# Retention of a hybrid decoder step, rewritten: states in four row groups, old states over four column groups, halves swapped by DMA, tables loaded earlier

## The reference, cut to what matters

```python
x1, x2 = xf[..., :half], xf[..., half:]                    # rotary, on q and k
return jnp.concatenate([x1 * c - x2 * s, x1 * s + x2 * c], axis=-1)
...
qk = jnp.einsum('bhid,bhjd->bhij', q, k) * dmask[None]
inner = jnp.einsum('bhij,bhje->bhie', qk, v)
cross = jnp.einsum('bhid,bhde->bhie', q, state) * jnp.exp(lg * (idx + 1.0))[None, :, :, None]
k_dec = k * jnp.exp(lg * (c_len - 1.0 - idx))[None, :, :, None]
new_state = jnp.exp(lg * c_len)[None, :, :, None] * state + jnp.einsum('bhjd,bhje->bhde', k_dec, v)
...
o_r = rmsnorm(o_r).reshape(b, s, RET_V_W) * jax.nn.silu(rg.astype(jnp.float32))
```

## Time and profile before

| | |
|---|---|
| three runs, median | 3351.26 us |
| profiled execution, its own time | 3356.02 us |
| its span (first to last instruction) | 3353.8 us |
| mean granted TensorE clock | 0.947 |
| PE busy | 3095.2 us (92%) |
| DVE busy | 1820.4 us (54%) |
| ACT busy | 1257.0 us (37%) |

### The profile page before, as it was taken

One profiled execution on the slowest core, in us unless ns is written; L12 is line 12 of the kernel. 1 busy time (PEld: TensorE's weight loads), 2 busy tenths in 40 slices (PEclk: granted clock), 3 DMA queues, 4 the chain that ended last, 5 costly groups with the idle time before them and its releaser, 6 DMA issues. The chain is left out here.

```text
span 3353.8 us, 52494 instructions
## 1 busy us (share of the span) xinstructions
PE 3095.2 (92%) x20972; PEld 2873.7 (86%) x20972; DVE 1820.4 (54%) x2531; ACT 1257.0 (37%) x1380; POOL 1016.0 (30%) x551
## 2 busy tenths in 40 slices
PE   7999999896887798599989999999999999999998
PEld 6999999674787686599989999999999888888886
DVE  5444443333222100565365889987777567777664
ACT  5322232111443334343334444445445333333332
POOL 0000000001454353000323888977777201111000
PEclk9999999666999899799989999999999999999999
DMA  6545453333447652466775789999999878888764
GB/s 218 173 157 175 151 174 100 114 101 125 133 149 242 221 161 90 136 212 200 193 158 138 187 225 241 233 254 294 281 294 278 315 283 318 289 314 318 277 226 163
DMA packets 446856, 696.74 MB, mean 208 GB/s; under 512 B 30493, under 2 KB 343101, under 8 KB 419166
## 3 DMA queue, kind: packets, MB, share of 16 engines
q1 hardware_dynamic: 397374, 554.41, 53.3%
q10 hardware_dynamic: 40128, 73.42, 7.9%
q0 software_dynamic: 9216, 67.11, 5.3%
HBM read 628.01 MB, written 63.70 MB: 206 GB/s over the span
## 5 line engine op out<-in xcount | busy, mean ns | idle before, releaser
L2506 POOL TENSOR_TENSOR peer_uT_low<-peer_uT,peer_uT_high 128x1024 fp32r<-128x1024 f32 x256 | 615.6, 2429 | 262.0 <-ACT peer_uT_high L2533 261.4
L968 POOL TENSOR_TENSOR gate_low<-gate_raw,gate_high 128x512 fp32r<-128x512 f32 x192 | 244.5, 1300 | 1073.8 <-ACT gate_high L924 1073.8
L2406 PE MATMUL banks<-x_high,peer_uT_high 128*128 128x256 f32 x2048 | 497.6, 285 | 7.0 <-ACT peer_picks_T L2565 5.1
L2407 PE MATMUL banks<-x_low,peer_uT_high 128*128 128x256 f32 x2048 | 493.4, 282 | 0.0
L2406 PEld LDWEIGHTS banks<-x_high,peer_uT_high 128*128 128x128 f32 x2048 | 389.9, 190 | 7.9 <-ACT peer_uT_high L2533 5.0
L2407 PEld LDWEIGHTS banks<-x_low,peer_uT_high 128*128 128x128 f32 x2048 | 389.2, 190 | 0.0
L228 PE MATMUL banks<-x_high,win_high 128*128 128x288 f32 (+1 forms) x1312 | 349.1, 296 | 0.0
L229 PE MATMUL banks<-x_low,win_high 128*128 128x288 f32 (+1 forms) x1312 | 348.7, 295 | 0.0
L198 ACT ACTIVATE win_high<-win_raw 128x2048 fp32r<-128x2048 f32 x84 | 160.8, 1915 | 334.0 <-DVEq L191 329.2
L2533 ACT ACTIVATE peer_uT_high<-peer_uT 128x1024 fp32r<-128x1024 f32 x256 | 260.5, 1055 | 63.3 <-DVE peer_uT L2656 62.6
L2656 DVE STREAM_TRANSPOSE peer_uT<-peer_u 128x1024 f32<-128x1024 f32 x192 | 234.1, 1230 | 84.1 <-DMA peer_u<-in_peer_u_dram 53.5
(11 more groups left out here) (398 smaller groups left out, 6688.5 us busy)
## 6 DMA issues: line engine op xcount, KB each, us to landing
win_raw<-in_w_in_dram SPq DMA_DIRECT2D x38, 2048.0 KB, 8.1
peer_u<-in_peer_v_dram SPq DMA_DIRECT2D x64, 1024.0 KB, 5.5
peer_area<-in_peer_v_dram SPq DMA_DIRECT2D x64, 1024.0 KB
gate_raw<-in_w_in_dram SPq DMA_DIRECT2D x96, 512.0 KB, 4.0
peer_u<-in_peer_u_dram SPq DMA_DIRECT2D x192, 256.0 KB
peer_u<-in_peer_u_dram ACTq DMA_DIRECT2D x192, 256.0 KB
w_raw<-in_w_up_ret_dram SPq DMA_DIRECT2D x8, 2048.0 KB, 8.9
w_raw<-in_w_out_dram SPq DMA_DIRECT2D x8, 2048.0 KB, 8.8
```

Of the source, the lines that this page charges most:

```text
L968: pool.tensor_tensor(self.low[:, p % 2, c, :, :], self.raw[:, p % 4, :, c * P:(c + 1) * P], self.high[:, p % 2, c, :, :], ALU.subtract).th ...
L2406: pe.matmul(out, UH[:, c, k, :], XH[:, k, 0:DENSE], start=(k == 0), stop=False)
L2407: pe.matmul(out, UH[:, c, k, :], XL[:, k, 0:DENSE], start=False, stop=False)
L2506: pool.tensor_tensor(UL[:, m % 2, part, :], UT[:, m % 2, part, :], UH[:, m % 2, part, :], ALU.subtract).then_inc(low, 1)
```

## The change

The output is the same. The changes are these:

1. The nine tables are loaded at the end of `input_projections` (SP, behind the last weight load) into `branch_outputs`, which is free until the next branch. The semaphores are no longer restarted in blocks of their own: POOL starts the rest of them during the input projection and renews the used ones during retention.
2. The silu of the gate runs at the end of ScalarE's part of the input projection.
3. Rotary: two DMAs a head copy q and k with their halves swapped into `SW`; VectorE multiplies by signed sines. There is no rotation matrix and no product for it. The factor on k goes into the decay tables.
4. v is turned straight from `Z`. The new tokens' k and v are turned four times into four groups of 32 output partitions, as ordinary products with the identity.
5. The old states become the moving operand (256 columns), q of the new tokens the stationary one (32 columns, zero but for the request's four). Four requests go to four column groups. The sum over requests needs a ScalarE copy (`CR`) and two small products with `pick`.
6. The new tokens' states run in four row groups of 32 partitions, each into its own bank, all eight before the first addition. The additions overwrite the old states in place; these are then stored, and the next load into that buffer waits for the store.
7. The root and the scaling are done head by head.
8. VectorE's order in head h is: the request's q (`QG`), the decayed keys (`KD`, `KDN`), the decayed scores (three pieces), the mean square of head h-1, the rotary sum of head h+1, the gate of head h, the four additions to the states, the scaling of head h-1. ScalarE copies the values (`V`, `V4`), `CR` and `PST`, squares the outputs, then takes the root of head h-1.
9. The heads are unrolled. PSUM banks 6 and 7 stay free, and the four first gate loads are issued at the start of retention. `TICKS_RETENTION` is (0, 0): no gate work runs in it.

```diff
+                def swap(h):
+                    if h >= 2:
+                        sp.wait_ge(qk_ready, after(h - 1))
+                    for half in range(2):
+                        sp.dma_start(SW[half * 64:half * 64 + 64, h % 2, :, :],
+                                     qk_z[64 - half * 64:128 - half * 64, h]).then_inc(swapped[h % 2], 16)
+                def load(h):
+                    if h >= 2:
+                        sp.wait_ge(new_stored[h % 2], after(16 * (h // 2)))
+                    sp.dma_start(ST[:, h % 2, :, :], state_in[h]).then_inc(state_loaded[h % 2], 16)
+                swap(0)
+                swap(1)
+                load(0)
+                gates.begin(sp)
+                load(1)
+                for h in range(RET_HEADS):
+                    gates.sp(sp, BEFORE)
+                    if h >= 1 and h + 1 < RET_HEADS:
+                        load(h + 1)
+                    if h + 2 < RET_HEADS:
+                        swap(h + 2)
...
+                def root(h):
+                    act.wait_ge(ms_ready, after(h + 1))
+                    act.activation(Z[:, RK + h, :], Z[:, RQ + h, :], ACT.Ln).then_inc(logs, 1)
+                    act.wait_ge(logs, after(h + 1))
+                    act.activation(Z[:, RV + 2 * h, :], Z[:, RK + h, :], ACT.Exp, scale=-0.5).then_inc(rstd_ready, 1)
+                for h in range(RET_HEADS):
+                    act.wait_ge(v_turned, after(h + 1))
+                    act.wait_ge(states_done, after(h))
+                    act.activation(V[:], PS[:, 1, :].rearrange("p (t e) -> p t e", t=2), ACT.Copy)
+                    act.activation(V4[:], PS[:, 2, 0:RET_DV], ACT.Copy).then_inc(v_ready, 1)
...
+                    act.wait_ge(cross_done, after(h + 1))
+                    act.activation(CR[:], PS[:, 0, 0:RET_DV], ACT.Copy).then_inc(cr_ready, 1)
+                    act.wait_ge(pstate_done, after(h + 1))
+                    act.wait_ge(pstate_stored, after(16 * h))
+                    act.activation(PST[:], PS[:, 1, 0:RET_DV], ACT.Copy).then_inc(pstate_ready, 1)
...
+                        root(h - 1)
+                    gates.act(act, BEHIND)
+                root(last_head)
+            @block.gpsimd
+            def _(pool):
+                gates.pool(pool, RET_HEADS * (BEFORE + BEHIND))
+                G["signals"].renew(pool, finished)
...
+                    dve.tensor_tensor(turned, turned, tables.sin.unsqueeze(1).to_broadcast([P, 2, T]), ALU.mult).then_inc(rope_parts, 1)
+                    dve.wait_ge(scores_done, after(h))
+                    dve.wait_ge(qg_ready, after(h))
+                    dve.tensor_tensor(QK[:], qk_z[:, h], tables.cos.unsqueeze(1).to_broadcast([P, 2, T]), ALU.mult).then_inc(rope_parts, 1)
+                    dve.wait_ge(rope_parts, after(2 * h + 2))
+                    dve.tensor_tensor(QK[:], QK[:], turned, ALU.add).then_inc(qk_ready, 1)
```

The products of a head, after (TensorE):

```diff
+                def turn_new(columns, source):
+                    for j in range(4):
+                        last = pe.matmul(PS[32 * j:32 * j + 32, columns[0], columns[1]:columns[1] + P], source, ident[:],
+                                         start=True, stop=True, skip_group_check=True)
+                    return last
+                def turn_values(h):
+                    pe.wait_ge(states_added, after(4 * h - 1))
+                    for e in range(2):
+                        source = Z[:, RV + 2 * h + e, :]
+                        for t in range(2):
+                            pe.transpose(PS[:, 1, t * RET_DV + e * P:t * RET_DV + (e + 1) * P], source[:, t * P:(t + 1) * P], ident[:])
+                        last = turn_new((2, e * P), source[:, SEQ:T])
+                    last.then_inc(v_turned, 1)
+                def turn_keys(h):
+                    pe.wait_ge(qk_ready, after(h + 1))
+                    for t in range(2):
+                        pe.transpose(PS[:, 0, t * P:(t + 1) * P], QK[:, 1, t * P:(t + 1) * P], ident[:])
+                    turn_new((0, 2 * P), QK[:, 1, SEQ:T]).then_inc(k_turned, 1)
+                def scores(h):
+                    pe.wait_ge(states_added, after(4 * h))
+                    pe.matmul(PS[:, 3, 0:SEQ], QK[:, 1, 0:P], QK[:, 0, 0:SEQ], start=True, stop=True)
+                    pe.matmul(PS[:, 3, SEQ:SEQ + P], QK[:, 1, P:SEQ], QK[:, 0, P:SEQ], start=True, stop=True)
+                    pe.matmul(PS[0:NEW, 3, SEQ + P:SEQ + P + NEW], QK[:, 1, SEQ:T], QK[:, 0, SEQ:T], start=True, stop=True).then_inc(scores_done, 1)
...
+                def cross(h):
+                    pe.wait_ge(kd_ready, after(2 * h + 2))
+                    pe.wait_ge(qg_ready, after(h + 1))
+                    pe.wait_ge(state_loaded[h % 2], after(16 * (h // 2) + 16))
+                    for r in range(2):
+                        for j in range(4):
+                            b = 4 * r + j
+                            last = pe.matmul(PS[32 * j:32 * j + 32, 0, 0:RET_DV], QG[:, b * NEW:(b + 1) * NEW], ST[:, h % 2, b, :],
+                                             start=(r == 0), stop=(r == 1), skip_group_check=True)
+                    last.then_inc(cross_done, 1)
...
+                        pe.matmul(PS[:, 4 + e, 0:SEQ], V[:, 0, es], PT[:, 0:SEQ], start=True, stop=False, skip_group_check=True)
+                        pe.matmul(PS[:, 4 + e, P:SEQ], V[:, 1, es], PT[:, SEQ:SEQ + P], start=False, stop=False, skip_group_check=True)
+                        pe.matmul(PS[:, 4 + e, SEQ:T], V4[0:NEW, es], PTN[:], start=False, stop=False, skip_group_check=True)
+                    pe.wait_ge(cr_ready, after(h + 1))
+                    for e in range(2):
+                        last = pe.matmul(PS[:, 4 + e, SEQ:T], CR[:, e * P:(e + 1) * P], tables.pick, start=False, stop=True, skip_group_check=True)
...
+                def states(h):
+                    pe.wait_ge(pstate_ready, after(h + 1))
+                    for r in range(2):
+                        for j in range(4):
+                            rows = slice(32 * j, 32 * j + 32)
+                            last = pe.matmul(PS[:, j, r * RET_DV:(r + 1) * RET_DV], KDN[rows, r, :], V4[rows, :],
+                                             start=True, stop=True, skip_group_check=True)
+                    last.then_inc(states_done, 1)
```

And the places around it (`decoder_step_kernel`, the input projection's SP, ACT and POOL, `diff_tables`, `attention`):

```diff
+    C["cos"] = const("c_cos", cos)
+    C["sin"] = const("c_sin", sin * np.where(np.arange(P) < half, -1.0, 1.0)[:, None])
...
+                for dst, src in tables.loads:
+                    sp.dma_start(dst, src).then_inc(tables_loaded, 16)
                 sp.wait_ge(spilled, after(16))
                 sp.wait_ge(stored, after(32))
+                sp.wait_ge(tables_loaded, after(16 * len(tables.loads)))
...
+                act.wait_ge(w.bank_free, after(2 + 4 * MEM_COUNT + RG + 2 * RET_HEADS))
+                for q in range(4):
+                    g = Z[:, RG + 4 * q:RG + 4 * q + 4, :]
+                    act.activation(g, g, ACT.Silu)
+            @block.gpsimd
+            def _(pool):
+                G["signals"].start_rest(pool)
...
-                gates.begin(sp)
...
+        finished = G["signals"].taken
         gates = GateStream(nc, G, outer, x_high, x_low)
+        retention(nc, G, Z, tables, gates, finished)
```

More of the change, by code:

```diff
@@ L88, in take, with start_rest, renew, clear @@
         self.taken += 1
+        if self.taken > len(self.sems):
+            assert self.taken - len(self.sems) <= self.renewed
+            return self.sems[self.taken - len(self.sems) - 1]
         assert self.taken <= self.started
         return self.sems[self.taken - 1]
+    def start_rest(self, pool):
+        for sem in self.sems[self.started:]:
+            pool.sem_inc(sem, START)
+        self.started = len(self.sems)
+    def renew(self, pool, count):
+        self.clear(pool, [s.num for s in self.sems[:count]])
+        for sem in self.sems[:count]:
+            pool.sem_inc(sem, START)
+        self.renewed = count
+    def clear(self, pool, numbers):
+        for first in [n for n in numbers if n - 1 not in numbers]:
+            last = first
+            while last + 1 in numbers:
+                last += 1
+            pool.sem_clear(range(first, last + 1))
     def from_zero(self, count):
@@ L99, in _ @@
             def _(pool):
-                numbers = [s.num for s in self.sems]
-                for first in [n for n in numbers if n - 1 not in numbers]:
-                    last = first
-                    while last + 1 in numbers:
-                        last += 1
-                    pool.sem_clear(range(first, last + 1))
+                self.clear(pool, [s.num for s in self.sems])
         self.taken = 0
@@ L110, in start @@
     def start(self, count):
-        self.started = count
+        self.started, self.renewed = count, 0
         def share(engine, k):
@@ L396, in sems, with __init__, table @@
         return [self.signals.take() for _ in names]
-def load_tables(nc, st, tables):
-    (loaded,) = st.sems("tables_loaded")
```

(39 more changed lines are left out.)

304 lines of the change are left out of this document (104 added, 200 removed).

## The result

| | us | ratio to before |
|---|---|---|
| before, median of 4 runs beside it | 3351.32 (3345.96 to 3353.88) | 1 |
| after, median of 4 runs | 3265.05 (3261.06 to 3276.63) | 0.975, interval 0.9723 to 0.9778 |
| forecast | 3260, range 3238 to 3300 | |

The profiled execution of after took 3276.63 us, the slowest of its four, with a span of 3274.8; the one of before took 3356.02. So 79.4 us went between these two, and 86 between the medians.

What follows compares the result with a forecast made beforehand. TensorE's own order of work was taken to bound the retention heads. Heads of 14 us (before 21.9) and shorter ends sum to 91 us less: 3356.0 to 3265, with the median 4.8 below, 3260 us; range 3238 to 3300.

Steps and rivals of the forecast that it cites:

- the clock: TensorE's granted clock in the retention heads, taken as 0.87, making a head 14 us where before it took 21.9.
- the stretch: From the input projection's last product to the bias tables' first product: 229.8 us before, forecast 91 us less.
- product end to the first head's states done: Retention's start: swaps, rotary sum, first state's load and first head's products, done 18.1 us after the input projection's end.
- seven heads: Retention's heads after the first head's states, at 14 us each: 98 us.
- tail to the next stage's first load: Retention's end: last additions, scaling of heads 6 and 7, mean square, root and semaphores, 10.4 us; before, 20.7.
- The signs: Profile marks expected: heads 14 us apart, clock 0.8 to 0.9, L680 about 2 us, a 2.8 us gap before L622.
- the rival without overlap in rows: New states' row groups don't overlap: products 3.6 to 4.2 us, 16 us a head, 3273; DMAs or rows together 0.10.
- The head at full clock: One retention head at clock 1: 2.8 us waiting for VectorE's additions plus 9.8 us of TensorE work, 12.6 us.
- The restart: Semaphore restart before retention, now gone, so retention may begin 1 us after 579.4; otherwise up to 6 us come back.
- ScalarE's roots: Each head's two table loads and small activations, 3.6 us behind the squares, claimed hidden at a margin of 1.2.
- slower: Rival: grouped products run one after another at clock 0.5, 35.6 us a head, 3423 us; chance 0.03.
- The changes of tiling mode: About ten TensorE drains a head from changed tiling; no more than a few hundredths, no cost borne out by the trace.

Runs made afterwards that it cites:

- e2_fill: The changed kernel with five 128x256 products on a free bank, results unread, ahead of TensorE's wait for the additions: 3245.41 us (one run).
- e5_own_block: The changed kernel with its tables loaded in a block of their own between input projection and retention, without a semaphore restart: 3268.98 us.
- e11_fill_no_root: e2_fill with ScalarE's logarithm and exponential of the root replaced by copies, without table loads: 3244.57 us.
- e4_col0: The changed kernel with all eight products with the old states sent to one column group: 3289.88 us.
- e7_no_root: The changed kernel with plain copies in place of the root's logarithm and exponential, without table loads: 3266.46 us.
- e8_no_wait: The changed kernel with v turned into free banks, old states' products in bank 2 not waiting for decayed keys, VectorE's scaling one head later: 3235.57 us, median of 5.
- e9_fill_row0: e2_fill with all eight state products of a head reading partitions 0 to 31, one row group instead of four: 3279.18 us.
- e10_fill_col0: e2_fill with the old states' products all sent to one column group instead of four: 3270.35 us.

## Why the prediction was right, and where it was not

It said 3260 us; the median is 3265.05. The direction, the order of work in a head and the places of the gain were right; the clock was not. That the number came so near is in part luck: for the profiled execution the working gives 3265, and it took 3276.63. The median then lay 11.6 us under that execution, where 4.8 were reckoned with. In the profiled execution the stretch lost 80.5 us of the 91 forecast, by these terms:

| | forecast | measured |
|---|---|---|
| product end to the first head's states done | 18.1 | 16.4 |
| seven heads | 98 | 111.7 |
| tail to the next stage's first load | 10.4 | 10.5 |
| bias tables | 12.2 | 10.6 |
| the stretch (before 229.8) | 138.7 | 149.25 |

- *The mis-sized term is the clock.* I took 0.87, between two stages of other make, from the share of time that TensorE would be busy. It was 0.76 over the heads, waits included. With the work of e2_fill, 2.5 + 10.23/0.76 is 15.96, the mean head (to the hundredth by chance, 0.76 being rounded); with 0.87 it would have been 14.3. That is 1.7 us in each of seven heads, 12 of the 13.7 us missed there. What I left out is the order: 2.4 us of idling in one piece, then half the clock for up to 7.7 us. That the busy share is no guide stood in my own rows: before, TensorE was busy 89% of the heads at a clock of 0.64.
- *The signs.* The first swap (0.90 us), the gap released by the additions (2.43), L652 without a wait for a load and the table loads ended before v is copied came as said; L680 was shorter than said (1.15, not 2). The heads (15.96, not 14, and outside the 13 to 15.5 that the forecast stood for) and the clock (0.76, not 0.8 to 0.9) did not. The length of a head alone would have fitted the rival without overlap in rows, which had 16 us; L680 decides against it, 1.15 us where that rival had 3.6 to 4.2.
- *The head at full clock* was forecast at 2.8 + 9.8 = 12.6; e2_fill has 12.73. Inside, errors cancelled. States in row groups took 1.07, not the 1.9 taken from the row of the 128x4 products, near the lower bound of 0.96. Turning took 2.17 instead of 1.5 (from 649.96 to 652.13 in e2_fill), but not because a piece was left out: 1.5 is six transposes at 0.12 and three rounds at 0.24. Each pair of transposes took 0.36 where 0.24 were reckoned, and each round over the column groups 0.36; scores, squares and outputs were 0.5 longer together. The wait was 2.43 to 2.50, not 2.8.
- *The restart* is what is left as the cause of the 7.7 us (e5_own_block: 6.8 of them), and retention began 0.9 us behind the product. The first head was 1.7 us faster than forecast.
- *ScalarE's roots* are hidden, with 1.5 us left in the tail (e11_fill_no_root).
- *The gain of the two groupings*: 2.6 us for the rows and a fall of the clock avoided, 2.46 for the columns. The rivals "no overlap" and "slower" are out by the products' own times to the next row, 3.64 us in one row group against 1.07 in four, and 3.57 in one column group against 1.00 in four; and the slowest try, e4_col0, was still 60 us under before.
- *DMAs*: a state's load landed in 6.3 us at the median, under the 7.8 of the earlier trace rows, and only the first head was held by a DMA (the swap, 2.87 us on VectorE). At 10.3 us a head the first such wait shows.
- *The changes of tiling mode.* The price of the rule in "TensorEngine Tiling (Array Packing)" of the Trainium skill, Key Properties, was put at nothing, from one row, and e2_fill does not bear that out. Its turning changes between the full array and four column groups behind every pair of transposes, and each of the six pieces takes 0.12 us more than its columns, 0.7 us a head (rows from 649.96 on, above). Where transposes follow one another without such a change, in before, 64 of them take 7.06 us to the next row, 0.11 each, against 0.18 here:

```profile
L2494 PE MATMUL banks<-ident,peer_area 128*128 128x128 f32 x64 | 7.3, 275 | 0.0
```

Whether the change itself or the weight loads at it take the time, no run separates.

- *Transposes and the clock.* The rule that transposes don't count for the clock ("TensorE: Matmul & The Clock Gate" of the Trainium skill, Part 4) did not decide it: with them in each head the clock was 1.00 in e2_fill. Before's own trace speaks against it, too: through those 64 transposes (3314.94 to 3322.00, nothing else on TensorE) the clock is 1.00, and for 8 us behind them.

The median of after lies 11.6 us under the profiled execution; that one has a rest at the top of what the kernels showed (2533 to 2545) and, if e5_own_block and e7_no_root are a measure, long heads. I can name what lowers the clock, but not how long it stays low: the same order and the same wait gave heads of 14.9 in one execution and 15.96 in another. That stays open. Not tested one by one are the silu's new place, the root head by head in place of all at once, and the restart.

## What to carry to other kernels

Price a wait on TensorE twice: its own length, and what runs at half clock behind it. Here 2.4 us of idling cost 3.2 us more in a head of 12.7, and five products that nobody reads gave them back. Waits of 0.7 us and less cost only themselves (e8_no_wait). Move the wait's cause first (another bank, another order of VectorE); two such moves (e8_no_wait) took 29 us off after's median.

Products over few partitions belong in four row groups where they can, here for their own time and for the clock behind them. And look at what stands between two stages: with the restart of the semaphores and the small tables there, TensorE had no work for 19 us.

## What I had not expected of the hardware

- The clock fell from 1.00 to 0.52 on a TensorE that was never idle, behind 3.6 us of products on 32 partitions in one row group (e9_fill_row0), and not behind as long a run of products in one column group (e10_fill_col0).
- Adding work made the kernel faster: stretch 149.3 to 125.6 us (e2_fill).
- Eight float32 products of 32 x 256 with sixteen weight loads of 128 columns end in 1.07 us over four row groups. The weight loads overlap like the products: each lasts 0.18 us, and the sixteen of one head together 0.74.
